# Two attentions of the second block: values as the stationary operand in two column halves, probabilities scaled before their transposes

## The reference

```python
# layer 0, "sparse": 16 heads of 64 share one key and one value head; per query the 64 best
# admissible keys by an indexer's score
logits = einsum('bqhd,bqkd->bhqk', q, k_gathered) * 64 ** -0.5
logits = where(valid, logits + rel_bias[bucket(key - query)], NEG)
out = einsum('bhqk,bqkd->bqhd', softmax(logits), v_gathered) @ w_o
# layer 1, "latent": 16 heads, keys of 96, values of 64, a mask by chunks of 64 tokens
logits = where(mask, einsum('bqhd,bshd->bhqs', q, k) * 96 ** -0.5, NEG)
out = einsum('bhqs,bshd->bqhd', softmax(logits), v) @ w_o
# after each: h = h + out; h = h + square(relu(rms(h) @ w_up)) @ w_down
```

## Time and profile before

| | us |
|---|---|
| median of three runs | 1713.62 |
| span of the profiled execution | 1711.1 |
| what lies between that span and the median | 2.5 |
| sparse attention, first scores to output product | 1179.6 to 1216.64 |
| latent attention, first scores to output product | 1469.4 to 1502.4 |
| PE busy over the span | 1397.3 (82%) |
| DVE, ACT, POOL busy over the span | 536.3, 389.7, 132.3 |

### The profile page before, as it was taken

One profiled execution on the slowest core, in us unless ns is written; L12 is line 12 of the kernel. 1 busy time (PEld: TensorE's weight loads), 2 busy tenths in 40 slices (PEclk: granted clock), 3 DMA queues, 4 the chain that ended last, 5 costly groups with the idle time before them and its releaser, 6 DMA issues.

```text
span 1711.1 us, 21197 instructions
## 1 busy us (share of the span) xinstructions
PE 1397.3 (82%) x8724; PEld 855.2 (50%) x8724; DVE 536.3 (31%) x899; ACT 389.7 (23%) x579; POOL 132.3 (8%) x108
## 2 busy tenths in 40 slices
PE   4999997676666667757766766898999999999999
PEld 2986542222122112212221221476899998989997
DVE  2785310000000000000000000058365557835554
ACT  3515200000000000000000000057443346843332
POOL 1430000000000000000000000004500000730000
PEclk8999988877878877787877787899999999999999
DMA  9777599999999999999999999992154544425552
GB/s 376 263 290 301 228 382 426 429 427 429 429 429 429 429 428 429 429 428 428 428 429 428 428 429 429 428 344 99 52 195 179 178 162 149 143 99 197 195 179 93
DMA packets 80325, 542.05 MB, mean 317 GB/s; under 512 B 6312, under 2 KB 9721, under 8 KB 52626
## 3 DMA queue, kind: packets, MB, share of 16 engines
q1 hardware_dynamic: 76912, 535.93, 76.8%
q0 software_dynamic: 1632, 5.03, 1.0%
q10 hardware_dynamic: 1730, 0.36, 0.1%
HBM read 540.22 MB, written 1.08 MB: 316 GB/s over the span
## 4 chain that ended last, share of the span: by engine, by line
PE 47%; DMA 47%; DVE 3%; ACT 1%; issue 1%; POOL 1%; SPq 0%; DVEq 0%; ACTq 0%; POOLq 0%
DMA ring<-in_w_down 22%; DMA ring<-in_w_up 21%; PE bank L1387 10%; PE bank L1389 10%; PE bank L1388 10%; PE bank L1754 4%; PE bank L1773 3%; PE bank L1640 2%; DMA ring<-in_a_w_in 2%; DMA ring<-in_w_mod 1%; DMA ring<-in_w_in 1%; PE bank L1423 1%; PE bank L1621 1%; PE bank L1561 1%; PE bank L1733 1%
## 5 line engine op out<-in xcount | busy, mean ns | idle before, releaser
L1754 PE MATMUL bank<-ring,low 128*32 128x512 f32 x2016 | 314.5, 769 | 152.1 <-DMA ring<-in_w_up 125.7
L1754 PEld LDWEIGHTS bank<-ring,low 128*32 128x32 f32 x2016 | 66.6, 130 | 381.0 <-DMA ring<-in_w_up 192.5
L1773 PE MATMUL bank<-ring,low 128*32 128x512 f32 x976 | 167.7, 822 | 93.7 <-DMA ring<-in_w_down 86.6
L1133 ACT ACTIVATE low<-bank 128x512 f32<-128x512 f32 x16 | 9.6, 597 | 844.8 <-PE bank L1754 844.8
L927 ACT ACTIVATE ring_parts<-ring 128x4096 fp32r<-128x4096 f32 (+3 forms) x46 | 151.9, 3301 | 205.8 <-DMA ring<-in_mlp_w_down 101.0
L2083 DVE TENSOR_TENSOR ring_parts<-ring,ring_parts 128x4096 fp32r<-128x4096 f32 (+2 forms) x35 | 148.5, 4244 | 141.0 <-ACT ring_parts L927 141.0
L1388 PE MATMUL bank<-feat_parts,ring_parts 128*128 128x256 f32 x640 | 181.6, 284 | 0.0
L1389 PE MATMUL bank<-feat_parts,ring_parts 128*128 128x256 f32 x640 | 181.6, 284 | 0.0
L1387 PE MATMUL bank<-feat_parts,ring_parts 128*128 128x256 f32 x608 | 173.4, 285 | 6.8 <-DVE feat_parts L2153 3.7
L2429 DVE TENSOR_TENSOR low<-low,bank 128x512 f32<-128x512 f32 x16 | 11.0, 688 | 462.4 <-PE bank L1754 462.4
L1773 PEld LDWEIGHTS bank<-ring,low 128*32 128x32 f32 x976 | 31.7, 131 | 210.2 <-DMA ring<-in_w_down 135.3
(11 more groups left out here) (407 smaller groups left out, 1979.9 us busy)
## 6 DMA issues: line engine op xcount, KB each, us to landing
ring<-in_w_gate SPq DMA_DIRECT2D x64, 2048.0 KB, 25.7
ring<-in_w_up SPq DMA_DIRECT2D x62, 2048.0 KB, 23.0
ring<-in_w_down SPq DMA_DIRECT2D x61, 2048.0 KB, 26.2
ring<-in_mlp_w_up SPq DMA_DIRECT2D x16, 2048.0 KB, 7.8
ring<-in_mlp_w_down SPq DMA_DIRECT2D x16, 2048.0 KB, 7.9
ring<-in_w_mod SPq DMA_DIRECT2D x11, 2048.0 KB, 15.5
ring<-in_w_in SPq DMA_DIRECT2D x3, 2048.0 KB, 13.3
ring<-in_a_w_in SPq DMA_DIRECT2D x3, 2048.0 KB, 16.1
```

The lines of the kernel that those rows point to most:

```text
L1754: last = pe.matmul((GATE if i < 4 else UP)[32 * j:32 * j + 32, :], xsT[:, k, :], held(n, 2)[:, kk, 512 * j:512 * j + 512], start=(k == 0), ...
L1773: last = pe.matmul(TURN[32 * g:32 * g + 32, :], hidT[:, c, 32 * j:32 * j + 32], down_row(n, c, d), start=(j == 0 and c < 2), stop=(j == 3 ...
```

## The change

In both attentions:

- DVE scales the probabilities themselves: once the exponentials of a step are there, it takes the reciprocals and multiplies the 2n columns of `pexp` in place (`scaled`). This is done one step ahead, scaled(i+1) in step i, scaled(0) before the loop. PE's T(i) waits for it instead of the exponential.
- The values become the stationary operand (128 keys x 64) and pT moves (128 columns). The first head's result goes to partitions 0 to 63 of the bank, the second's to 64 to 127. So the result is feature-major at once; it fills the bank X(j) itself, two steps to a bank. The multiplication of results (L2290), the token-major buffers' writes, the O banks and the X transposes are gone.
- ACT's high part and DVE's low part of X(j) move one step ahead of before. In the sparse attention they write with a reversed last dimension, in place of the reversed identity.
- The banks of both attentions have fixed homes by a formula.

In the sparse attention bias and maximum become one instruction per head, which adds the strip, negates, writes back and takes the minimum; the exponential is then taken with scale -1.

```diff
@@ ACT
-                    if i >= 3 and i % 2:
-                        high_out((i - 3) // 2)
+                    if i >= 2 and i % 2 == 0:
+                        high_out((i - 2) // 2)
@@ PE
+                def outputs(i):
+                    out, nb = bk(f"{pre}X{i // 2}")[:, P * (i % 2):P * (i % 2 + 1)], tile_step(i)[0] + 1
+                    pe.wait_ge(*drained(f"{pre}T{i}"))
+                    if i % 2 == 0:
+                        banks.wait_free(pe, f"{pre}X{i // 2}")
+                    for b in range(nb):
+                        for h in range(2):
+                            last = pe.matmul(out[HD * h:HD * (h + 1), :], values(i, h, b), pT[i % 4][:, h * nb + b, :],
+                                             start=(b == 0), stop=(b == nb - 1), skip_group_check=True)
+                    if i % 2:
+                        end(last, f"{pre}X{i // 2}")
...
-                        pe.wait_ge(*drained(f"{pre}S{i}"))
+                        pe.wait_ge(sem(pre + "_scaled"), i + 1)
...
-                        for h in range(2):
-                            for b in range(nb):
-                                last = pe.matmul(bk(f"{pre}O{i - 1}")[:, HD * h:HD * (h + 1)], pT[(i - 1) % 4][:, h * nb + b, :],
-                                                 outputs(i - 1, h, b), start=(b == 0), stop=(b == nb - 1))
-                        end(last, f"{pre}O{i - 1}")
-                    if i >= 3 and i % 2:
-                        turn_out((i - 3) // 2)
+                    if i:
+                        outputs(i - 1)
@@ DVE
-                def output(i):
-                    dve.wait_ge(*drained(f"{pre}S{i}"))
-                    link(dve.reciprocal(at_r[:, i % 4, :], at_s[:, i % 4, :]))
-                    dve.wait_ge(*banks.filled(f"{pre}O{i}"))
-                    first = HD * head_at(i, 0)
-                    dve.tensor_tensor(split(token_out[:, i // 8, first:first + 2 * HD], 2), split(bk(f"{pre}O{i}")[:, 0:2 * HD], 2),
-                                      at_r[:, i % 4, :].unsqueeze(2).to_broadcast([P, 2, HD]), ALU.mult)
+                def scaled(i):
+                    n = tile_step(i)[1]
+                    dve.wait_ge(*drained(f"{pre}S{i}"))
+                    link(dve.reciprocal(at_r[:, i % 4, :], at_s[:, i % 4, :]))
+                    p = split(pexp[i % 3][:, 0:2 * n], 2)
+                    dve.tensor_tensor(p, p, at_r[:, i % 4, :].unsqueeze(2).to_broadcast([P, 2, n]), ALU.mult)\
+                        .then_inc(sem(pre + "_scaled"), 1)
...
                 maxima(0)
                 maxima(1)
+                scaled(0)
                 for i in range(N_AT):
                     if i + 2 < N_AT:
                         maxima(i + 2)
-                    if i:
-                        output(i - 1)
-                    if i >= 4 and i % 2 == 0:
-                        low_out((i - 4) // 2)
+                    if i + 1 < N_AT:
+                        scaled(i + 1)
+                    if i >= 3 and i % 2:
+                        low_out((i - 3) // 2)
...
-            def sa_bias(i, s):
+            def sa_maximum(i):
                 t, n, _ = tile_step(i)
-                link(dve.tensor_tensor(s, s, strips[:, pair_heads(i), P * (1 - t):P * (1 - t) + n], ALU.add))
+                for h in range(2):
+                    s = bk(f"saS{i}")[:, n * h:n * (h + 1)]
+                    last = dve.tensor_tensor_reduce(s, s, strips[:, head_at(i, h), P * (1 - t):P * (1 - t) + n], -1.0, -NEG,
+                                                    ALU.add, ALU.min, at_m[:, i % 4, h:h + 1])
+                return last
```

More of the change, by code:

```diff
@@ L528, in two_blocks, with pair_groups, fill, scores @@
         group("q2T0", "q2T1", among=unscored)
[L530 to L538, removed]
+        def pair_groups(pre, beside):
+            first = (banks.last + 1) % 8
+            def fill(name, home):
+                group(name, among=[(first + home) % 8])
+            def scores(i):
+                fill(f"{pre}S{i}", i if i < 3 else (4, 2)[i - 3] if i < 5 else (4, 0, 1, 2)[(i - 5) % 4])
+            for i in range(2):
+                scores(i)
+            for i in range(N_AT + 1):
                 if i + 2 < N_AT:
-                    fill(f"{pre}S{i + 2}")
+                    scores(i + 2)
                 if i < N_AT:
-                    fill(f"{pre}T{i}")
-                if 0 < i <= N_AT:
-                    fill(f"{pre}O{i - 1}")
-                if i >= 3 and i % 2:
-                    fill(f"{pre}X{(i - 3) // 2}")
-                fill(*beside.get(i, ()))
+                    fill(f"{pre}T{i}", 3 if i == 0 or i >= 4 and i % 2 == 0 else 5)
+                if i % 2:
+                    fill(f"{pre}X{i // 2}", 6 + i // 2 % 2)
+                for name, home in beside.get(i, ()):
+                    fill(name, home)
         LATE_QUERIES = 0
-        pair_groups("sa", {LATE_QUERIES: ("q2T2", "q2T3")})
+        pair_groups("sa", {LATE_QUERIES: (("q2T2", 6), ("q2T3", 7))})
         out_groups("ao", wo2)
@@ L579, in query_turn @@
             eng.tensor_tensor(qr, qr, rot, ALU.add).then_inc(sem("q3"), 1)
-        steps = ((1, "O0", 0), (1, "q4", 6), (1, "q5", 7), (1, "q6", 1), (1, "q7", 3), (2, "S4", 2), (2, "T2", 5), (2, "O1", 0),
[3 rows of a table removed]
-        home = {("q3T" if g[0] == "q" else "la" + g[0]) + g[1:]: b for _, g, b in steps}
-        pair_groups("la", {LATE_TURN: [f"q3T{i}" for i in range(4, 8)]}, home)
+        pair_groups("la", {LATE_TURN: tuple(zip((f"q3T{i}" for i in range(4, 8)), (7, 0, 1, 3)))})
         out_groups("bo", wo3)
@@ L1035, in attend_local, with attend_pairs @@
                 output(N_NA - 1)
-            def attend_pairs(pre, parts_out, between=None, scale=None, beside=None):
+            def attend_pairs(pre, parts_out, scale, between=None, beside=None):
                 def exp(i):
@@ L1043, in exp @@
                         last = act.activation(pexp[i % 3][:, h * n:(h + 1) * n], bk(f"{pre}S{i}")[:, h * n:(h + 1) * n],
-                                              ACT.Exp, bias=at_m[:, i % 4, h:h + 1], scale=scale(i, h) if scale else 1.0,
+                                              ACT.Exp, bias=at_m[:, i % 4, h:h + 1], scale=scale(i, h),
                                               accum_out=at_s[:, i % 4, h:h + 1])
@@ L1322, in la_scale @@
                 return qs[2][:, n:n + 1]
-            attend_pairs("la", boT, None, la_scale, la_beside)
+            attend_pairs("la", boT, la_scale, beside=la_beside)
             weights_high(first_mlp[1])
@@ L1585, in attend_local, with attend_pairs @@
                         local_turn(j - 2)
-            def attend_pairs(pre, scores, outputs, token_out, order, between=None):
+            def attend_pairs(pre, scores, values, between):
                 def score_group(i):
@@ L1591, in score_group @@
                     scores(i)
[L1593 to L1601, removed]
+                def outputs(i):
[7 more added lines that the diff above has]
+                                             start=(b == 0), stop=(b == nb - 1), skip_group_check=True)
+                    if i % 2:
+                        end(last, f"{pre}X{i // 2}")
                 score_group(0)
                 score_group(1)
-                for i in range(N_AT + 2):
+                for i in range(N_AT + 1):
                     if i + 2 < N_AT:
```

60 lines of the change are left out of this document (21 added, 39 removed), and 3 rows, old and new, of the table steps.

## The result

| | before | after |
|---|---|---|
| median | 1713.46 us (4 runs) | 1721.89 us (4 runs, 1719.83 to 1724.04) |
| ratio of the runs | | 1.0048, 95% interval 1.0036 to 1.0061 |
| span of the profiled execution | 1711.1 | 1718.8 |
| sparse attention, first scores to output product | 37.1 | 39.0 |
| latent attention | 33.1 | 38.0 |

The kernel became slower by 8.4 us, against 6.0 forecast (1719.6). Of the 7.7 us between the spans 2.0 arose in the sparse attention and 5.0 in the latent one. What lies between the two attentions takes 252.7 us in both kernels, what follows 208.7 and 209.0.

What follows compares the result with a forecast made beforehand. PE was taken to bound the kernel, with a thin lead inside the attentions. Latent +5.6 and sparse +0.4 made +6.0 on the 1711.1 us span; carrying over 2.5 to the median gave 1719.6, 8-in-10 range 1706 to 1729.

Steps and rivals of the forecast that it cites:

- sparse second tile: Sparse attention, five second-tile steps: about 2.45 us each against 2.51, -0.3 in all (bounds -2.0 and +3).
- sparse steps 0 to 3: Sparse attention's first steps: POOL idle, fusion saves what scaling costs, 0 us (bounds -0.5 and +0.5).
- latent opening: Latent attention's start up to S4: three scalings stand before DVE's late-query copy, +2.4 us (bounds +1.0 and +4).
- The wait that decides: Scaling with both operands in SBUF waits for POOL's instruction: 0.62 us sparse, 0.5 latent on average, at most 1.27.
- Latent first tile: Latent steps 2 to 7: DVE needs 1.87 us a step against 1.44, +2.4 in all (bounds -0.1 and +4).
- Second tile: Latent attention, five steps: a rhythm with POOL gives 2.45 us against 2.18, +1.3 (bounds -1.2 and +3.3).
- Tail: End of each attention: result scaling and transposes go, last transposes wait for scaling, net -0.5 us (bounds -1.4, +0.3).
- Values on PE: Second-tile value groups in overlapping column halves: 0.7 us, PE saves 0.25 a step (gain 0.5 to loss 0.35).
- Rival 2: Both attentions: value halves do not overlap, 0.88 + 0.2 us a group, +3 in all, 1722.6; chance 0.10.
- I price no clock change: Both attentions: granted clock 1.00 (2.4 GHz level), PE over nine tenths busy, so no clock cost counted.
- Rival 1: Both attentions: port waits land in slack and PE's saving shows, -5.0 us, 1708.6; chance 0.28.
- Rival 3: Both attentions: effects cancel, port waits 0.2 to 0.3 us, PE gain half used, 1713.6 within 3; chance 0.12.

Runs made afterwards that it cites:

- small_pieces: Changed kernel with POOL's splits of the output weights in pieces of 256 columns in place of 512: 1717.34 us, ratio 1.0029.
- unscaled: Changed kernel with the scaling cut to one column of each head, the rest of the normalisation left out: 1717.28 us, ratio 1.0029.
- recip_bank: Changed kernel with reciprocals written into the step's score bank (except steps 2 and 3), so scaling has one bank operand: 1715.56 us, ratio 1.0018.
- pool_by_dma: Changed kernel with DMA copies in place of POOL's splits of the output weights, leaving POOL nearly idle: 1714.87 us, ratio 1.0009.
- rb_clock: recip_bank plus products of the identity that fill PE's gaps before first-tile transposes in both attentions: 1715.78 us, ratio 1.0012.
- no_scaling: Changed kernel without reciprocals and scalings; transposes wait for the exponentials alone, normalisation left out: 1706.77 us, ratio 0.9968.
- rb_head_order: recip_bank with second-tile value products ordered by head in place of alternating column halves: 1716.48 us, ratio 1.0016.
- mixed: Sparse attention as in recip_bank, latent attention in its old form: 1712.10 us, ratio 0.9993 to the kernel before.

## Why the prediction was right

The forecast was +6.0, the spans differ by +7.7 and the medians by 8.4. The mechanism that it named, a scaling in front of the transposes that waits for POOL, is shown by the experiments. How near the number came is in part luck, since misses offset each other: of its terms one has the wrong sign (sparse second tile), one was missed (sparse steps 0 to 3), and the latent opening reached its size by another route.

- **The wait that decides** was named rightly and nearly sized: 0.46 on top of 0.69 in the sparse second tile (0.62 taken), 0.21 in the latent one and 0.27 in its first (0.5 taken). Removed from either side, by a bank operand or by an idle POOL, it gives back some 6 us of 8.4. The Trainium skill, "SBUF — State Buffer", section Terms, makes the shared port pair exclusive for the full instruction. small_pieces and unscaled agree (978 for 1149 with half the piece, and 455 for a product of 160).
- **Latent opening**: +3.0 for +2.4, by another sum. I had three port waits of 0.5; the three scalings took 0.42, 0.77 and 0.69, so 0.6 in all. I counted DVE's work ahead of the query copies. The chain goes through the key copies of step 0: the first values (O0) are written to the bank from which DVE still has to copy key 6, and the late turn to that of key 7. Those copies start 4.6 us after S0, 2.5 before the change, since the first exponential, its reciprocal and two scalings now stand in front of them: +2.0. The late turn itself adds 1.1, by the clock (below). Without port waits +2.2 (recip_bank) and +2.0 (pool_by_dma) remain, both with a fall of the clock, and +1.8 without a fall (rb_clock), so my low bound of +1.0 was wrong.

```profile
1475.66 0.77 DVE brow L2271
1476.43 0.67 DVE feat L2726
...
1477.23 0.70 PE bank L1598 x4
1477.93 3.07 PE bank L1995 x16
```

- **Latent first tile**: +2.5 for +2.4, but again without port waits +1.0 (both experiments), where I had -0.1. **Second tile**: +0.7 for +1.3; the first two steps took 2.45 each, as the rhythm had it, the last three 2.23 (S12 at 1496.76, S15 at 1503.46), with PE alone on the chain. **Tail**: -1.3 for -0.5, near the bound.
- **Sparse**: steps 0 to 3 (S0 to S4) +1.1 for 0, and 4 to 7 +0.6 for +1.2. Of the first, 0.6 is there without any scaling (no_scaling 6.1, before 5.5) and 0.7 in recip_bank: the fixed homes put S4 into S2's bank, so PE's S4 waits for the exponential of step 2. The bank homes stood nowhere in my sum. The wait of the scores in no_scaling (1178 to 1190), which the kernel before doesn't have there, is shown below. Second tile +0.9 for -0.3: with waits of up to 1.05 on a scaling, DVE came onto the chain. Tail -0.6 for -0.5. The fused pair costs 0.73 from start to start, not 0.96, so DVE had more room than I gave it, and the port took that too.

```profile
PEld bank L1852 <- ACT brow L1042: 1.5, 2, 0.8
```

- **Values on PE**: 0.59 for 0.7 a group, a step of 2.31 where PE leads (no_scaling, recip_bank) for 2.51: the saving of 0.2 was sized nearly (0.25) for the wrong reason. The rounds in two halves don't overlap to any gain; serial ones cost 0.074 an instruction and not 0.11. Rival 2 was right in its premise, no overlap, and wrong in its price, a serial 0.88. The Trainium skill, "TensorEngine Tiling (Array Packing)", Key Properties, says that a change of mode drains the TensorE. Here the whole group of eight with both changes takes 0.59, and twice 0.24 would leave 0.11 for eight instructions, so no drain of that size is there.
- **"I price no clock change"** failed: 1477 to 1480 ran at 0.50, the 1.2 GHz level, behind waits of 1.45 and 0.72 of PE for the scaling. The late turn (16 loads) took 2.88 there and 1.77 before: 1.1 of the opening's 3.0.

```profile
1477.00:1480.00 3.00, 2.77 (x14) 2.37 (x15) 2.82 (x8) 1.33 (x5) 2.92 (x3) 0.50 0.00 0
```

Rival 1 (1708.6) had the premise that only the port stands between the change and PE's gain. With the port out of the way it is 1715; a time below the kernel before comes only when the scaling is gone. Rival 3 (it cancels, 1713.6) had port waits of 0.2 to 0.3, which is what the latent attention shows, but the time lies 8 us above it.

## What to carry to other kernels

A DVE instruction with all its operands in SBUF, beside a POOL that works back to back, costs its own length plus a wait up to one POOL instruction, however short it is; give it one operand in a bank, or cut POOL's pieces. Before work is moved in front of PE's transposes, count the latency it adds to the first steps of a stage, not only the engine's busy time, and what else on that engine it pushes back (here the key copies). Give new bank homes a term of their own in the sum. Parts of a change that pay can hide the price of another: measure the form without it.

## What was not expected of the hardware

- Value instructions in column halves gain nothing from alternating halves (rb_head_order); with a 64-column stationary tile and 128 moving columns one is issued every 0.074 us, in either order, against 0.105 for a 128-column tile with 64 moving.
- The granted clock fell to the 1.2 GHz level in the latent attention of six of the nine profiled kernels with the new form there, and in the sparse one of four of the eleven with the new form there; in none of the old form, and in none with the gaps filled. In mixed it came right behind 2 us in which PE was busy for 0.86, and S8 to S9 took 3.2 us where recip_bank took 1.9. Yet recip_bank had nearly the same gap (0.95 in 1191 to 1193) and kept 1.00, so such a gap doesn't decide alone. What does is open.
- DVE's fused add and minimum over 256 columns takes 0.44 plus 0.14 to read the accumulator, and two of them 0.73 together, less than the plain add (0.70) and maximum (0.69) of 512 that they replace.
